# Hybrid attention encoder on Trainium2: the scaling of the first attention's probabilities split over three engines

## What is computed

```python
def attend(q_blk):
    logits = jnp.einsum("bqkgd,bskd->bkgqs", q_blk, k).astype(jnp.float32) * scale
    p = jax.nn.softmax(logits, axis=-1).astype(v.dtype)
    return jnp.einsum("bkgqs,bskd->bqkgd", p, v)
```

## Time and profile before

| | |
|---|---|
| median of 3 runs | 2730.91 us (2730.24 to 2731.38) |
| the profiled execution, its own time | 2732.0 us |
| its span, first to last instruction | 2730.2 us |
| busy: PE, DVE, ACT, POOL | 2648.5, 1290.5, 1039.5, 894.8 us |
| mean granted PE clock | 0.994 of full speed |
| first attention, between its ends | about 138 to 259 us and 1477 to 1597 us |

### The profile page before, as it was taken

The page is one execution under the profiler, slowest core; times in us unless marked ns, Lnnn a source line. Parts: engine busy times, 40 slices in busy tenths (PEclk is TensorE's granted clock), DMA queues, the critical chain, the costliest instruction groups (busy, mean ns, idle before and its releaser), DMA issues.

```text
span 2730.2 us, 36378 instructions
## 1 busy us (share of the span) xinstructions
PE 2648.5 (97%) x13796; PEld 2221.2 (81%) x13796; DVE 1290.5 (47%) x2694; ACT 1039.5 (38%) x2138; POOL 894.8 (33%) x634
## 2 busy tenths in 40 slices
PE   6999999999999999999999999999999999999998
PEld 4788878878888888878897878888888888888787
DVE  3576275722344355542346734575224343555223
ACT  3386114711344534521225831175024445354111
POOL 2274341024243342123423734200334342422232
PEclk9999999999999999999999999999999999999999
DMA  5100111021111231111420011100211113211122
GB/s 175 33 9 18 49 45 30 1 54 39 47 46 44 67 91 47 32 39 43 159 69 15 9 37 48 45 11 1 70 40 51 47 43 94 64 39 34 45 101 92
DMA packets 201415, 138.02 MB, mean 51 GB/s; under 512 B 20968, under 2 KB 187496, under 8 KB 201208
## 3 DMA queue, kind: packets, MB, share of 16 engines
q1 hardware_dynamic: 187420, 129.21, 16.7%
q10 hardware_dynamic: 13824, 6.49, 0.8%
HBM read 120.77 MB, written 19.10 MB: 51 GB/s over the span
## 4 chain that ended last, share of the span: by engine, by line
PE 89%; DVE 5%; ACT 4%; issue 2%; DMA 0%; POOL 0%; SPq 0%; ACTq 0%; POOLq 0%; DVEq 0%
PE ps L955 24%; PE ps L918 10%; PE ps L920 10%; PE ps L919 10%; PE ps L1160 5%; PE ps L1106 4%; PE ps L1125 3%; PE ps L1018 3%; PE ps L1019 3%; PE ps L1020 3%; PE ps L1080 3%; PE ps L1081 2%; PE ps L1091 2%; ACT prob L1458 1%; PE ps L1398 1%
## 5 line engine op out<-in xcount | busy, mean ns | idle before, releaser
L2275 POOL CAST wh<-wraw 128x1024 fp32r<-128x1024 f32 (+3 forms) x150 | 167.7, 1118 | 1553.6 <-PE ps L920 790.3
L918 PE MATMUL ps<-xh,wh 128*128 128x512 f32 x1088 | 427.2, 393 | 2.2 <-ACT pt_split L1682 2.2
L920 PE MATMUL ps<-xh,wl 128*128 128x512 f32 x1088 | 424.2, 390 | 0.0
L919 PE MATMUL ps<-xl,wh 128*128 128x512 f32 x1088 | 423.8, 390 | 0.0
L2277 POOL TENSOR_TENSOR wl<-wraw,wh 128x1024 fp32r<-128x1024 f32 (+3 forms) x150 | 396.1, 2641 | 12.1
L955 PE MATMUL ps<-xh,wh 128*128 128x512 f32 x896 | 366.4, 409 | 3.2 <-ACT att L1480 1.2
L955 PE MATMUL ps<-xh,wl 128*128 128x512 f32 x896 | 357.1, 399 | 0.0
L955 PE MATMUL ps<-xl,wh 128*128 128x512 f32 x896 | 356.4, 398 | 0.0
L1512 ACT ACTIVATE gs<-ps 128x512 f32<-128x512 f32 x96 | 57.0, 598 | 520.4 <-PE ps L920 515.9
L918 PEld LDWEIGHTS ps<-xh,wh 128*128 128x128 f32 x1088 | 204.7, 188 | 44.4 <-ACT pt_split L1682 3.0
L920 PEld LDWEIGHTS ps<-xh,wl 128*128 128x128 f32 x1088 | 204.5, 188 | 43.0
(11 more groups left out here) (294 smaller groups left out, 5218.2 us busy)
## 6 DMA issues: line engine op xcount, KB each, us to landing
wraw<-in_w_in_dram SPq DMA_DIRECT2D x128, 512.0 KB, 3.9
acc<-in_x_dram SPq DMA_DIRECT2D x16, 512.0 KB, 7.8
wraw<-in_w_branch_dram SPq DMA_DIRECT2D x64, 128.0 KB, 4.0
wraw<-in_w_out_dram SPq DMA_DIRECT2D x16, 512.0 KB, 3.5
dil_out<-cst ACTq DMA_DIRECT2D x96, 66.0 KB, 1.6
toep<-toep_row SPq DMA_DIRECT2D x16, 256.0 KB
xres<-acc SPq DMA_DIRECT2D x8, 512.0 KB, 2.6
acc<-xres SPq DMA_DIRECT2D x8, 512.0 KB, 7.0
```

The costliest lines, as they stand in the source:

```text
L918: pe.matmul(dst, ah, bh, start=i == 0, stop=False)
L919: pe.matmul(dst, ah, bl, start=False, stop=False)
L920: last = pe.matmul(dst, al, bh, start=False, stop=i == len(ks) - 1)
L2275: inc(pool.tensor_copy(high, raw), w_hi[l])
```

## The change

The first half of each unit's probabilities is itself divided: DVE scales keys 0 to 255 right after it has made the reciprocal, waiting for that reciprocal first, and ACT scales keys 256 to 511. POOL's part, keys 512 to 1023, stays. PE waits for both scalings before it transposes the first half.

```diff
+        quarter_scaled = each_layer("quarter_scaled")
...
+        QUARTER = S // 4
...
                 def transposes_part(s, part):
                     if s < b_u0:
                         pe.wait_ge((first_scaled, second_scaled)[part][l], s + 1)
+                        if part == 0:
+                            pe.wait_ge(quarter_scaled[l], s + 1)
...
                                 act.wait_ge(sums_set[l], x + 1)
-                                some = units[x]["prob"][:, 0:HALF]
+                                some = units[x]["prob"][:, QUARTER:HALF]
                                 inc(act.activation(some, some, ACT.Copy, scale=rs[:, c:c + 1]), first_scaled[l])
...
                         if later and begun(s - 1):
                             sum_inverse(s - 1)
+                            dve.wait_ge(sums_set[l], s)
+                            some, c = units[s - 1]["prob"][:, 0:QUARTER], (s - 1) % U_MAX
+                            inc(dve.tensor_scalar(some, some, rs[:, c:c + 1], None, ALU.mult), quarter_scaled[l])
                         if paired(s - 5):
```

## The result

| | before | changed |
|---|---|---|
| median of six runs each, in turns on one chip | 2730.57 us | 2741.22 us |
| lowest and highest | 2728.88, 2734.38 | 2738.40, 2745.47 |
| own time of the profiled execution | 2732.0 | 2738.4, its lowest |

The ratio is 1.0035, with a 95% interval of 1.0025 to 1.0045: slower by 10.65 us. That interval is 6.8 to 12.3 us, so the result lies inside the range given, and that it comes within 0.3 us of the forecast is closer than these runs can tell.

What follows compares the result with a forecast made beforehand. Bound: PE's waits in a loop of engines, where DVE's string up to T1 sets the cycle. Mean cycle 7.28 against 6.93 us, 28 x 0.36 = 10.1 us on the 2730.91 us median: 2741 us, range 2730 to 2760.

Steps and rivals of the forecast that it cites:

- T0: PE's four transposes of a row block's first half, right behind the value product; the forecast cycle starts there.
- T1: PE's transposes of the second half; they need the bank freed by DVE's first subtraction of the rest, 0.84 us after it starts.
- ACT's loop: Second loop: transposes, copy, scaling of the first half, exponential, logits; under 6.82 us minus 0.21, no longer deciding.
- short and long: Two alternating cycles of a pair of units, 6.82 and 7.03 us before, forecast at 7.16 and 7.40.
- ACT's relief: ACT scales 256 columns, not 512: 0.215 us less before each exponential, but no gain once DVE is later.
- wait at the logits: PE's weight load ahead of the logits waited 0.36 us on ACT; forecast to show no wait on ACT.
- odd step: There DVE's new scaling precedes one rest and falls into 1.40 us of DVE idle time: cost taken as 0.
- DVE ahead of POOL: New DVE scaling starts 0.20 us after the reciprocal, POOL's 0.25; DVE keeps its time, POOL ends 0.2 to 0.3 later.
- rival with POOL first: POOL's scaling takes the memory path before DVE's: 2780 us (chance 0.12) or, in a milder variant, 2758 us (0.07).
- gentle form: DVE's scaling is let in 0.55 us after POOL's start: 0.6 us more per cycle, 2758 us, chance 0.07.
- hard form: DVE's scaling waits until POOL's whole scaling ends: 1.41 us more per cycle, 2780 us, chance 0.12.
- ends of the attention: Start and finish of each layer's first attention, counted as one more cycle's loss of 0.36 us per layer.

Runs made afterwards that it cites:

- spare scaling: Changed kernel, but DVE writes its scaling to an unused buffer and ACT scales all 512 columns as before: 2744.85 us, ratio 1.0056 to the kernel before.
- relief alone: Changed kernel without DVE's scaling and PE's wait for it: ACT scales keys 256 to 511, nobody 0 to 255; 2726.87 us, ratio 0.9990 to before.
- even units only: Changed kernel, but DVE scales the quarter of even units alone and ACT all 512 columns of odd ones: 2729.34 us, ratio 0.9994 to before.
- control: Changed kernel plus one small waited-for DVE reciprocal behind the new scaling, which still starts ahead of POOL's: 2748.68 us, ratio 1.0067 to before.
- run with POOL first: Changed kernel plus one small waited-for DVE reciprocal ahead of the new scaling, which so starts behind POOL's: 2758.16 us, ratio 1.0109 to before.

## Why the prediction was right

**The bound** was the right one: a loop from T0 through ACT's copy and DVE back to T1, with ACT's loop just below. By its own steps, against the timeline of after:

| step | forecast | measured |
|---|---|---|
| reciprocal to the first rest, short and long | 0.80, 1.01 us | 0.79, 1.03 |
| that rest's start to T1 | 0.84 | 0.82, 0.84 |
| T1 to T0 | 2.35, 2.38 | 2.37, 2.38 |
| T0 to the reciprocal | 3.17 | 3.16 |
| cycle, mean | 7.28 | 7.29 |

**ACT's relief** was forecast at nothing once DVE is later. The spare scaling shows this: with and without relief the cycle is 7.29. Before DVE is later I gave it 0.06 us in every second cycle; the relief alone brought 0.08 us in each second one and nothing in the others. The wait at the logits did not vanish, as I wrote, but 0.15 us of it stayed in places, with no effect on T1.

**The odd step** was taken as free. This is shown by the run with even units only, and within the changed kernel, where from 181 to 210 us scalings of 0.90 and 0.35 us alternate in the odd steps and the cycles stay between 7.26 and 7.31. Even 1.26 us were free in the control. The limit shows in the two cycles of 8.24 us.

**DVE ahead of POOL**, by 0.05 us read off other instructions, was 0.06. POOL's delay was 0.16 us, less than the 0.2 to 0.3 given. The rival with POOL first was priced from the right rows in its gentle form, 2758 forecast and 2758.16 when forced. So close a match is partly luck: the scaling ended 1.07 us after the reciprocal, not 1.15, the cycle was 7.82 us, not 7.88, and the filling of the loop cost more than was allowed for. The hard form, which I held the likelier of the two, did not occur in even steps. By the rule of the Trainium skill, "SBUF — State Buffer", section "Who interferes with whom", it should have with POOL first: the one that issues first keeps the shared ports for its whole instruction. The measurement decides: DVE was done 0.82 us into a POOL scaling of 1.56 us in the even steps, and was held to the end only in some of the odd steps in which it had already been waiting behind another POOL instruction.

**The ends of the attention** are the part that was wrong in its make-up, and its sum came out by luck. I gave each layer one more cycle's loss, 0.36 us, beside 13. Layer 2, whose first logits start at 1477.34 us before and 1481.24 after, and whose last sum starts at 1597.8 and 1606.7 us, splits into 18.9 and 19.9 us up to the first sum, 83.2 and 87.5 for twelve cycles, 18.4 and 18.2 for the rest. So the filling of the loop cost 1.0 us, and the draining gained 0.2, which is ACT's relief: the relief alone drains in 18.1 us too, and the spare scaling, without relief, in 18.4 (layer 1). In sum 5.1 us for the layer, 10.1 for two if layer 1 did the same, by 28 x 0.36 = 10.1 forecast and 10.65 measured. Layer 1 of the kernel before can't be used for this: in its profiled execution PE's granted clock was 0.80 from 130 to 145 us, and 1.00 in that of after, and layer 1 there fills in 20.2 us. In part for the same reason the two spans differ by 6.4 us only; the mean granted clock was 0.994 before and 0.998 after. The 1.0 us of the filling can be divided by the relief alone, which fills in 18.4 us: the relief gives 0.45 us and DVE's scaling with PE's wait for it takes 1.5. That 1.5 us is more than 0.36 per cycle because two of the first five scalings last 0.9 and 1.1 us there, beside POOL's splits, I only argue.

## What to carry to other kernels

In a loop of engines, ask which instruction stands between the last thing an engine waits for and the next thing another engine waits for it. Work put there costs its whole length, however idle the engine is on average, and the same work half a step later can be free. Relief of an engine that shares the bound with another is worth next to nothing until the other is shortened too; here an output that nobody waited for stood ahead of one that PE did wait for, and moving it gave more than the division of labour. Before you put an SBUF to SBUF instruction on DVE beside a POOL one, see which of the two starts first, to a few hundredths of a microsecond. And a busy share near 100% is no proof of the bound: here PE showed as busy for 81.72 of 82.00 us over twelve cycles that another run did in 79.40.

## What the runs showed of the hardware that I had not expected

A DVE scaling of 128x256 that starts 0.13 us into a POOL scaling of 128x512 ends 0.82 us after POOL's start, and POOL's time is unchanged at 1.56 us. If it has to wait behind POOL's split of 96x256, three outcomes show, and they follow the time by which the split had started before the DVE scaling. At 0.18 us or less DVE gets in between the split and POOL's scaling and takes 0.90 us. At 0.18 to 0.23 us it is held until 0.15 or 0.16 us after the end of POOL's scaling, 2.20 to 2.25 us in all: three times in the control, twice with the spare place. At 0.29 to 0.30 us POOL's scaling gets in first as well, but DVE ends 0.83 us after its start, 1.25 to 1.26 us in all: four times in the control, once with even units only. The source view of the new scaling in the run with POOL first, and then in the control:

```profile
L2029 DVE TENSOR_SCALAR prob<-prob,rs x44: 353/694/1078, 141.5 to 1611.8; 128x256 f32<-128x256 f32 x44
L2029 DVE TENSOR_SCALAR rope_b<-rope_b,rs x20: 687/695/872, 147.0 to 1604.0; 128x256 f32<-128x256 f32 x20
```

```profile
L2028 DVE TENSOR_SCALAR prob<-prob,rs x44: 352/354/2252, 143.7 to 1610.1; 128x256 f32<-128x256 f32 x44
L2028 DVE TENSOR_SCALAR rope_b<-rope_b,rs x20: 352/354/2199, 149.3 to 1602.6; 128x256 f32<-128x256 f32 x20
```

Why that gap decides stays open; no run here sets it on purpose, and at 0.18 us, one hundredth being the step of the view, both of the first two outcomes occur (225.31 and 1514.58 of the control). Where DVE is first in an even step, POOL bears 0.16 or 0.17 us (1.72 or 1.73 for 1.56), less than the 0.35 us of the DVE instruction.
